# Joined read and update blocks of sample units, and a last output tile in two column groups

## Chip, cores and metric

The kernel runs as one program on the eight cores of one Trainium2 chip, written with instructions for each engine: TensorE (PE), VectorE (DVE), ScalarE (ACT), GpSimd (POOL) and the DMA queues of SyncE (SP) and GpSimd. Each core handles one of the eight prompt sequences and 16 of the 128 sample sequences; the cores don't talk to each other. The metric is the device time of the slowest core in microseconds.

## The reference

One inference step of a decoder trunk of two layers, for new prompts (2,048 tokens each, 16 learned tokens ahead of them) and for running samples (4 new tokens each). Cut to what matters:

```python
def run_layer(h, prompt, S0, ...):
    xn = rmsnorm(h, norm_g)
    q, k, v, ga, u, gb, alow, mg = jnp.split(xn @ w_in, IN_OFFSETS, axis=-1)
    la = log_sigmoid(alow @ w_alpha + b_alpha) / GATE_TAU
    # samples: one chunk of 4 tokens, starting from the stored state S0 (heads, 128, 256)
    o, S_new = gla_scan(q, k, v, la, S0, L)
    o = silu(ga) * gain * o * rsqrt(mean(o * o) + EPS)        # per head
    ya, yb = o @ w_a, (pool_mix(u) * silu(gb)) @ w_b
    s_a, s_b = split(sigmoid(mg + b_merge))
    return h + (s_a * ya + s_b * yb) @ w_out, S_new, buf_new

def gla_chunk_step(S, chunk):                                 # b: cumulated log-forget
    o = (masked q k^T with decay) @ v + (q * exp(b)) @ S      # the product with S: "read"
    S_new = exp(b_last) * S + (k * exp(b_last - b))^T @ v     # "update"

y = rmsnorm(h_last, final_norm_g)                             # after the second layer
```

The outputs are the normalised tokens of prompts and samples, and the new states of both layers.

## The kernel before

**Two phases in each layer.** Phase 1 makes the projections, the linear attention and the pooling branch of the prompt, in pairs of 128-token tiles (eight pairs; a ninth "pair" number 8 holds the 64 sample tokens and 16 learned tokens). Phase 2 goes over the pairs once more: `merge(l, j, c)` computes one of eight 128-feature chunks of the gated sum of both branches (28 matmuls of 128x128 by 256 tokens, in two PSUM banks), and `out_tile(l, j, i)` multiplies a 128-token tile by `w_out` (16 matmuls of 512 columns, in a pair of banks), adds the residual and normalises. In layer 1 it also writes the output `y`.

**The sample units.** The stored states of the 16 samples of a core are handled in phase 2, in eight units per layer; a unit takes two heads of four samples (1 MB). `sample_cast` makes a bf16 copy `S_bfm` of the loaded state (ScalarE, in two halves) and masks the keys into `kdm` (GpSimd). `sample_read` has eight matmuls, 128 rows by 32 columns by 256, four side by side in different column groups, all into the bank `bo` that four units share. `sample_write` takes four banks, runs eight matmuls of 32 rows by 128 columns by 256 (row group r into bank r), lets VectorE form `S_in * decay + bank` in eight instructions, stores the new state and asks for the load of unit u + 2.

**What sets the order.** The instructions of all engines are emitted in one list, and a planner (`Sched.list_schedule`) turns it into a queue for each engine: it runs through time with modelled costs, and each engine takes the instruction with the lowest number among those whose predecessors are done in the model. Dependencies are tracked by SBUF regions and by PSUM bank. Every engine then executes its queue strictly in that order and waits at semaphores. The sample work is cut into a list `units`; in `phase2`, after merge number k, entries are emitted as long as

```python
while done < len(units) and done * total < (k - 12) * len(units):   # total = 46
```

The list has 28 entries: opening, then cast, reads and write of eight units, two output entries, one gating entry. Banks come from `banks.one()` and `banks.pair()`, which hand out what was freed longest ago in the order of emission. Merges are numbered k = 6 to 71; of each pair from the third on, the merges c = 1 and c = 3 are followed by an output tile of the pair before.

**The end.** The last tile of layer 1 is the 64 sample tokens alone (`p == NPAIR`): 16 matmuls of 64 columns by 512 into two banks, then in two halves of 512 features on 64 partitions the residual sum, the squares with their sum, the product with the gain `fg`, then the power -1/2, the scaling (one half on ScalarE, one on VectorE) and two stores. SP closes with a wait for each DMA semaphore. Its first seven feature chunks `m3[:, kc]` may be multiplied before the last chunk's merge is through.

Lines in the profile are those of helpers: L537 is every matmul, L543 a transpose, L564 ScalarE's activation, L579, L586, L591 and L598 tensor_tensor, tensor_scalar, scalar_tensor_tensor and copies, L611 a DMA.

Of the kernel before, what the change touches and what calls it, by code (L numbers as in the profile page):

```python
# [13 lines left out]
D = 1024  # L14
# [362 lines left out]
def build_nc():  # L377
# [18 lines left out]
    gf_d = din("gfull", [NL + 1, 128, D])  # L396
    cf_d = din("cf", [128, NCF])

    y_d = dout("y", [NS + SEQ, D])
# [12 lines left out]
    with contextlib.ExitStack() as st:  # L412
# [5 lines left out]
        def f32(off, n):  # L418
            return arena[:, off // 4:off // 4 + n]
# [75 lines left out]
        bm_ = f32(v2_off + 10240, 912)  # L495
        gf = f32(v2_off + 38912, 1024)
        xnP_m = bf(v2_off + 34048, 1024)
        kd_m = bf(v2_off + 36096, 512)
# [33 lines left out]

        def mm(out, lhsT, rhs, start, stop, sgc=False, share=1.0):
            c = max(fsz(rhs) / 2.4 / share + 2.5, 28.0)
            if lhsT.dtype == F32:
                c *= 4.0
            return S.add("pe", lambda e: e.matmul(out, lhsT=lhsT, rhs=rhs, start=start, stop=stop,  # L537
                                                  skip_group_check=sgc),
                         r=[lhsT, rhs], w=[out], cost=c, lat=250.0, attach=True)

# [676 lines left out]

        def sample_read(u, bo):
            hp, j = divmod(u, 4)
            for i in range(2):  # L1220
                for r in range(4):
                    q_ = q_bd[:, (j * 4 + 2 * hp + i) * 128 + 32 * r:(j * 4 + 2 * hp + i) * 128 + 32 * r + 32]
                    mm(bank(bo)[32 * r:32 * r + 32, i * 256:(i + 1) * 256], q_,
                       S_bfm[:, (2 * r + i) * 256:(2 * r + i + 1) * 256], j + i == 0, False, sgc=True, share=4.0)

        def sample_write(l, u):
            hp, j = divmod(u, 4)
            bs = [banks.one() for _ in range(4)]
            for i in range(2):
# [81 lines left out]
        def load_h(l, k):  # L1311
            if k < 17:
                t = P2_TILES[k]
                r0, n = rows(t)
                src = hin if l == 0 else H1
                dma(hb[k % 3][0:n, :], src[r0:r0 + n, :], r=[("H1", t)] if l else [])

        def out_tile(l, j, i):
# [5 lines left out]
            m3 = V(mgT[j % 2], 8, N)  # L1324
            Wo = RR[:, (8 - N_EARLY_C) * CB:(8 - N_EARLY_C) * CB + 8192]
            h = hb[k % 3][0:n, :]
            b_ = banks.pair()
# [4 lines left out]
            y0 = 0 if t == 16 else r0 - NMETA  # L1332
            if l == 0 or p < NPAIR:
                stt(h, bank(b_)[0:n, :], 0.5, h, ALU.mult, ALU.add)
                banks.free(b_)
                if l == 0:
                    dma(H1[r0:r0 + n, :], h, w=[("H1", t)])
                    if p == NPAIR:
                        norm_t(1, h, n, k, V(xnT_m, 8, NM), True)
                    else:  # L1340
                        norm_t(1, h, n, k, V(xnO, 8, N)[:, :, i * 128:i * 128 + n])
                        if i == 1:
                            dma(XN[1][p], xnO, w=[("XN", 1, p)])
                else:
                    rs = rms(h, n, k)
                    stt(h, h, rs, fg[0:n, :], ALU.mult, ALU.mult)
                    dma(y_d[y0:y0 + n, :], h)
                load_h(l, k + 3)
                return
            s_ = ss[k % 3]  # L1350
            halves = [slice(b * 512, (b + 1) * 512) for b in range(2)]
            for b, c in enumerate(halves):
                stt(h[:, c], bank(b_)[0:n, c], 0.5, h[:, c], ALU.mult, ALU.add)
                act(xb[k % 2][0:n, c], h[:, c], AF.Square, scale=D ** -0.5, accum_out=s_[0:n, b:b + 1])
            banks.free(b_)
            hf = hb[(k + 1) % 3][0:n, :]
            for c in halves:
                tt("dve", hf[:, c], h[:, c], fg[0:n, c], ALU.mult)
            ts("dve", s_[0:n, 2:3], s_[0:n, 0:1], s_[0:n, 1:2], s2=EPS, op0=ALU.add, op1=ALU.add)
            tt("pool", s_[0:n, 3:4], s_[0:n, 2:3], nhalf[0:n, 0:1], ALU.pow)  # L1360
            for b, c in enumerate(halves):
                if b:
                    ts("dve", hf[:, c], hf[:, c], s_[0:n, 3:4])
                else:
                    act(hf[:, c], hf[:, c], AF.Copy, scale=s_[0:n, 3:4])
                dma(y_d[y0:y0 + n, c], hf[:, c])

        def phase2(l):
            dma(fg, gf_d[l + 1])
            for k in range(3):  # L1370
                load_h(l, k)
            units = [sample_open]
            box = {}

            def reads(u):
                if u % 4 == 0:
                    box[0] = banks.one()
                sample_read(u, box[0])

            for u in range(8):  # L1380
                units.append(lambda u=u: sample_cast(l, u))
                units.append(lambda u=u: reads(u))
                units.append(lambda u=u: sample_write(l, u))
                if u % 4 == 3:
# [104 lines left out]
```

How the kernel before makes its waits and increments, by code:

```python
            def run_engine(ename, eng):  # L251
                seen = {}
                for op in ops:
                    if op["eng"] != ename:
                        continue
                    need = {}
                    for d in op["kept"]:
                        sk, val = ops[d]["token"]
                        if need.get(sk, 0) < val:
                            need[sk] = val
                    items = [(sk, val) for sk, val in need.items() if seen.get(sk, 0) < val]
                    attach = items.pop() if (items and op.get("attach")) else None
                    for sk, val in items:
                        eng.wait_ge(sems[sk], val)
                        seen[sk] = val
                    inst = op["fn"](eng)
                    if attach is not None:
                        inst._wait_ge(sems[attach[0]], attach[1])
                        seen[attach[0]] = attach[1]
                    if op["token"] is not None:
                        sk, val = op["token"]
                        inst.then_inc(sems[sk], 16 if op["dma"] else 1)
                if ename == "sp":
                    for k, v in sorted(self.dma_final.items(), key=lambda kv: self.last_use[kv[0]]):
                        sk = ("dma",) + k
                        if seen.get(sk, 0) < v:
                            eng.wait_ge(sems[sk], v)
```

## Time and profile before

| what | value |
|---|---|
| time, median of 3 runs (lowest, highest) | 1153.65 us (1151.91, 1154.72) |
| the profiled execution: time | 1150.47 us |
| its span on the slowest core (core 3) | 1148.9 us |
| spans of the eight cores | 1144.4 to 1148.9 us |
| mean granted TensorE clock of the cores | 0.992 to 0.994 |
| PE busy | 1113.7 us, 97% |
| DVE, ACT, POOL busy | 610.0, 516.0, 597.9 us |

A span runs from the first to the last instruction of a core; the time of an execution holds a little more. Rows below come from the slowest core, in us from the span's start. PE is the matmul, PEld the load of its weights, which runs ahead of it.

### The profile page before, as it was taken

Reading aid. Unit: us, or ns where it says so; the run is one execution under the profiler, and the core shown is the slowest. Engines: PE = TensorE matmul, PEld = TensorE weight load, DVE = VectorE, ACT = ScalarE, POOL = GpSimd, SP = SyncE. Lnnn points to the kernel's source line nnn. Section 1 sums busy time; section 2 is a strip of 40 time slices with the busy share of each in tenths; the row PEclk is TensorE's granted clock in tenths of the full one; section 3 lists DMA queues with packets and bytes.
Section 4 is the critical chain, followed back from the end, with each engine's and each line's share of the span. In section 5 each row is a group of like instructions: output and inputs, shape, how many; then the busy total and the mean of one; then the engine's idle time right before and its main releaser. Section 6 shows DMA issues by size and latency. Waiting matters only on the chain.

```text
span 1148.9 us, 27473 instructions; the slowest of 8 cores (1144.4 to 1148.9 us)
## 1 busy us (share of the span) xinstructions
PE 1113.7 (97%) x9990; PEld 860.8 (75%) x9990; DVE 610.0 (53%) x927; ACT 516.0 (45%) x1052; POOL 597.9 (52%) x903
## 2 busy tenths in 40 slices
PE   7899999999999999999999999999999999999997
PEld 3587777777788777777767877787788777777774
DVE  5457767665642544436344776756665254544534
ACT  2545566665432333434237366555543233333333
POOL 5159788866943333333342887778785233232232
PEclk8999999999999999999999999999999999999999
DMA  9956657775697899998689224454568866655531
GB/s 191 194 110 139 137 95 150 152 159 90 94 221 146 240 276 248 249 234 223 169 162 205 56 74 90 86 84 96 99 103 195 156 197 210 222 187 172 162 102 58
DMA packets 123991, 179.06 MB, mean 156 GB/s; under 512 B 82448, under 2 KB 88976, under 8 KB 119760
## 3 DMA queue, kind: packets, MB, share of 16 engines
q1 hardware_dynamic: 108592, 141.26, 43.6%
q0 software_dynamic: 15264, 36.05, 21.9%
q8 instruction: 78, 1.28, 0.5%
q14 instruction: 57, 0.47, 0.2%
HBM read 139.87 MB, written 54.59 MB: 169 GB/s over the span
## 4 chain that ended last, share of the span: by engine, by line
PE 85%; DMA 7%; issue 2%; ACT 2%; POOL 2%; DVE 1%; SPq 0%; POOLq 0%; ACTq 0%; DVEq 0%
PE psum L537 84%; DMA arena<-sgla 2%; DMA arena<-w 2%; ACT arena L564 2%; DMA arena<-hin 2%; POOL arena L579 1%; DMA nsg_s<-arena 1%; DVE arena L591 1%; DVE arena L579 1%; POOL arena L586 0%; PE psum L543 0%; ACT L564 0%; DVE arena L586 0%; POOL arena L598 0%; SPq L611 0%
## 5 line engine op out<-in xcount | busy, mean ns | idle before, releaser
L537 PE MATMUL psum<-arena 128*128 128x256 bf16 (+6 forms) x9886 | 1109.5, 280 | 23.9 <-DMA arena<-w 6.0
L537 PEld LDWEIGHTS psum<-arena 128*128 128x128 bf16 (+2 forms) x9886 | 854.8, 98 | 273.7 <-issue 32.1
L579 POOL TENSOR_TENSOR arena<-arena 128x256 bf16<-128x256 f32 (+15 forms) x349 | 347.5, 1001 | 268.9 <-DVE arena L591 220.1
L591 DVE SCALAR_TENSOR_TENSOR arena<-arena,psum 128x256 f32<-128x256 f32 (+7 forms) x472 | 266.8, 600 | 295.4 <-PE psum L537 140.4
L564 ACT ACTIVATE arena<-psum,arena 128x256 f32<-128x256 f32 (+3 forms) x432 | 173.2, 457 | 274.0 <-PE psum L537 223.1
L586 POOL TENSOR_SCALAR arena<-arena 128x256 f32<-128x256 f32 (+6 forms) x378 | 165.2, 445 | 189.9 <-ACT arena L564 120.0
L564 ACT ACTIVATE arena<-psum 128x256 bf16<-128x256 f32 (+5 forms) x258 | 159.2, 631 | 184.8 <-PE psum L537 157.7
L564 ACT ACTIVATE arena<-arena 128x1024 bf16<-128x1024 f32 (+5 forms) x144 | 142.5, 1001 | 151.7 <-DVE arena L591 103.5
L591 DVE SCALAR_TENSOR_TENSOR arena<-arena 128x256 bf16<-128x256 f32 (+4 forms) x124 | 117.1, 952 | 53.2 <-POOL arena L579 52.2
L591 DVE SCALAR_TENSOR_TENSOR arena<-psum,arena 128x256 bf16<-128x256 f32 (+6 forms) x125 | 92.3, 760 | 78.4 <-PE psum L537 73.7
L611 POOL DMA_DIRECT2D arena<-w x106 | 62.4, 591 | 38.5 <-POOL arena L579 13.5
L579 DVE TENSOR_TENSOR arena<-psum,arena 128x512 bf16<-128x512 f32 (+4 forms) x64 | 55.1, 868 | 38.3 <-PE psum L537 22.4
L598 POOL COPY arena<-arena 128x4 f32<-128x4 f32 (+3 forms) x64 | 27.9, 442 | 48.2 <-ACT arena L564 37.0
L564 ACT ACT_TABLE_LOAD x30 | 38.5, 1283 | 18.6 <-PE psum L537 16.3
L814 DVE TENSOR_TENSOR_SCAN arena<-arena 128x1024 f32<-128x1024 bf16 (+1 forms) x18 | 39.5, 2196 | 13.1 <-ACT arena L564 13.0
L586 DVE TENSOR_SCALAR arena<-psum,arena 128x256 bf16<-128x256 f32 x64 | 28.0, 478 | 28.3 <-POOL arena L579 23.7
L564 ACT ACTIVATION_READ_ACCUMULATOR arena<-psum 128x1 f32 x136 | 27.1, 200 | 0.0
L598 DVE CAST arena<-psum 128x256 bf16<-128x256 f32 (+1 forms) x18 | 7.2, 402 | 15.8 <-PE psum L537 15.5
L543 PE MATMUL psum<-arena 128*128 128x128 bf16 (+1 forms) x104 | 8.6, 224 | 3.5 <-POOL arena L598 2.9
L543 PEld LDWEIGHTS psum<-arena 128*128 128x128 bf16 (+1 forms) x104 | 6.8, 102 | 6.1 <-POOL arena L598 3.5
L586 DVE TENSOR_SCALAR arena<-arena 128x1024 bf16<-128x1024 f32 (+6 forms) x13 | 6.6, 516 | 8.4 <-POOL arena L579 4.6
L564 ACT ACTIVATION_READ_ACCUMULATOR arena<-arena 128x1 f32 (+2 forms) x52 | 9.8, 188 | 0.0
(9 smaller groups left out, 15.0 us busy)
## 6 DMA issues: line engine op xcount, KB each, us to landing
arena<-hin SPq DMA_DIRECT2D x32, 512.0 KB, 6.9
arena<-sgla SPq DMA_DIRECT2D x16, 1024.0 KB, 8.0
nsg_s<-arena SPq DMA_DIRECT2D x16, 1024.0 KB, 8.0
arena<-w POOLq DMA_DIRECT2D x30, 512.0 KB, 14.9
arena<-w POOLq DMA_DIRECT2D x48, 224.0 KB, 5.7
arena<-XN SPq DMA_DIRECT2D x20, 512.0 KB, 6.8
H<-arena SPq DMA_DIRECT2D x16, 512.0 KB, 4.1
arena<-H SPq DMA_DIRECT2D x16, 512.0 KB, 4.4
```

What stands on the lines that cost most here:

```text
L537: return S.add("pe", lambda e: e.matmul(out, lhsT=lhsT, rhs=rhs, start=start, stop=stop, skip_group_check=sgc), r=[lhsT, rhs], w=[out], co ...
L543: return S.add("pe", lambda e: e.transpose(out, in_, ident), r=[in_, ident], w=[out], cost=c, lat=250.0, attach=True)
L564: return S.add("act", lambda e: e.activation(out=out, in_=in_, func=func, **kw), r=r, w=w, cost=c)
L579: return S.add(eng, lambda e: e.tensor_tensor(out=out, in0=in0, in1=in1, op=op), r=[in0, in1], w=[out], cost=c)
L586: return S.add(eng, lambda e: e.tensor_scalar(out=out, in0=in0, **kw), r=r, w=[out], cost=ecost(eng, fsz(out), 0.55, [out] + r))
L591: return S.add("dve", lambda e: e.scalar_tensor_tensor(out=out, in0=in0, scalar=scalar, in1=in1, op0=op0, op1=op1), r=r, w=[out], cost=eco ...
L598: return S.add(eng, lambda e: e.tensor_copy(out=out, in_=in_), r=[in_], w=[out], cost=ecost(eng, fsz(out), 0.55, (out, in_)) + (500.0 if e ...
L611: return S.add(eng, lambda e: e.dma_start(out=out, in_=in_, **kw), r=list(r) + sb_r, w=list(w) + sb_w, dma=True, after=after, cost=nb / rate)
L814: S.add("dve", lambda e: e.tensor_tensor_scan(out=B, data0=rm[:, 0:4 * n], data1=A, initial=0.0, op0=ALU.mult, op1=ALU.add), r=[rm[:, 0:4 ...
```

## The change

The read and the update of a sample unit become one entry, `sample_step`: it takes the four banks first, then emits the eight reads and the eight updates. The first read is told to the planner as also reading the whole `S_bfm` and the masked keys `kdm`, and as also writing all four update banks, so the later 15 matmuls hang on it. The list `units` has 20 entries instead of 28.

The last output tile of layer 1 gets a function of its own. The 1,024 features are halved over the partitions: features 0 to 511 of the 64 tokens on partitions 0 to 63, 512 to 1,023 on partitions 64 to 127. The matmuls are 32 of 64 columns by 256, in turn for column groups 0 to 63 and 64 to 127, in two quarters q with a bank each. The sums of squares of both partition halves are added by two FP32 matmuls with a constant 128x128 matrix `pr` that is a new input (ones where the token is the same). The residual of that tile and the final gain are loaded in the same halved layout, the gain into the region of phase 1's first weights. Scaling is by ScalarE for partitions 0 to 63 and VectorE for 64 to 127, and two stores write `y`.

```diff
+        fgl, pair_f = f32(0, 512), f32(2048, 128)
...
-        def mm(out, lhsT, rhs, start, stop, sgc=False, share=1.0):
+        def mm(out, lhsT, rhs, start, stop, sgc=False, share=1.0, also_r=(), also_w=()):
...
-                         r=[lhsT, rhs], w=[out], cost=c, lat=250.0, attach=True)
+                         r=[lhsT, rhs] + list(also_r), w=[out] + list(also_w), cost=c, lat=250.0, attach=True)
...
-        def sample_read(u, bo):
+        def sample_step(l, u, bo):
+
             hp, j = divmod(u, 4)
+            bs = [banks.one() for _ in range(4)]
+            first = dict(also_r=[S_bfm, kdm[u % 2]], also_w=[bank(b) for b in bs])
             for i in range(2):
                 for r in range(4):
                     q_ = q_bd[:, (j * 4 + 2 * hp + i) * 128 + 32 * r:(j * 4 + 2 * hp + i) * 128 + 32 * r + 32]
                     mm(bank(bo)[32 * r:32 * r + 32, i * 256:(i + 1) * 256], q_,
-                       S_bfm[:, (2 * r + i) * 256:(2 * r + i + 1) * 256], j + i == 0, False, sgc=True, share=4.0)
-
-        def sample_write(l, u):
-            hp, j = divmod(u, 4)
-            bs = [banks.one() for _ in range(4)]
+                       S_bfm[:, (2 * r + i) * 256:(2 * r + i + 1) * 256], j + i == 0, False, sgc=True, share=4.0, **first)
+                    first = {}
             for i in range(2):
                 h = 2 * hp + i
                 for r in range(4):
...
+                if t == 16 and l:
+                    for x in range(2):
+                        dma(hb[k % 3][64 * x:64 * x + 64, 0:512], src[0:NS, x * 512:(x + 1) * 512], r=[("H1", t)])
+                    return
...
+            if l and p == NPAIR:
+                return last_tile(m3, Wo, k)
...
+        def last_tile(m3, Wo, k):
+
+            h, hf, s_ = hb[k % 3][:, 0:512], hb[(k + 1) % 3][:, 0:512], ss[k % 3]
+            cs = [slice(q * 256, (q + 1) * 256) for q in range(2)]
+            for q, c in enumerate(cs):
+                b_ = banks.one()
+                for kc in range(8):
+                    for x in range(2):
+                        w_ = kc * 1024 + x * 512 + q * 256
+                        mm(bank(b_)[64 * x:64 * x + 64, 0:256], m3[:, kc, :], Wo[:, w_:w_ + 256], kc == 0, kc == 7, sgc=True,
+                           share=2.0)
+                stt(h[:, c], bank(b_)[:, 0:256], 0.5, h[:, c], ALU.mult, ALU.add)
+                act(xb[k % 2][:, c], h[:, c], AF.Square, scale=D ** -0.5, accum_out=s_[:, q:q + 1])
                 banks.free(b_)
...
+                tt("dve", hf[:, c], h[:, c], fgl[:, c], ALU.mult)
+            b_ = banks.one()
+            for q in range(2):
+                mm(bank(b_)[:, 0:1], pair_f, s_[:, q:q + 1], q == 0, q == 1)
+            ts("dve", s_[:, 2:3], bank(b_)[:, 0:1], EPS, op0=ALU.add)
             banks.free(b_)
...
+            tt("pool", s_[:, 3:4], s_[:, 2:3], nhalf[:, 0:1], ALU.pow)
+            o0, o1 = hb[k % 3][0:64, 512:1024], hb[(k + 1) % 3][64:128, 512:1024]
+            act(o0, hf[0:64, :], AF.Copy, scale=s_[0:64, 3:4])
+            ts("dve", o1, hf[64:128, :], s_[64:128, 3:4])
+            dma(y_d[0:NS, 0:512], o0)
+            dma(y_d[0:NS, 512:1024], o1)
...
+            if l:
+                for x in range(2):
+                    dma(fgl[64 * x:64 * x + 64, :], gf_d[l + 1, 64 * x:64 * x + 64, x * 512:(x + 1) * 512])
+                dma(pair_f, pr_d[:, :])
...
-                units.append(lambda u=u: reads(u))
-                units.append(lambda u=u: sample_write(l, u))
+                units.append(lambda u=u: step(u))
```

## Rows read from the trace of the kernel before

**Rows 1.** The page, busy time of the engines: us (share of the span) xinstructions.
```profile
PE 1113.7 (97%) x9990; PEld 860.8 (75%) x9990; DVE 610.0 (53%) x927; ACT 516.0 (45%) x1052; POOL 597.9 (52%) x903
```

**Rows 2.** Windows; stretch: us; PE, PEld, DVE, ACT, POOL busy (x); PEclk; DMA share; GB/s.
```profile
320.00:575.00 255.00, 254.39 (x2194) 198.71 (x2192) 111.32 (x169) 87.60 (x186) 86.72 (x134) 1.00 0.86 222
...
915.00:1111.00 196.00, 194.37 (x1606) 145.17 (x1607) 88.21 (x136) 68.25 (x142) 55.52 (x81) 1.00 0.54 178
1111.00:1149.00 38.00, 29.70 (x386) 22.26 (x383) 15.42 (x24) 12.68 (x35) 9.88 (x19) 0.92 0.21 72
```

**Rows 3.** PE's waits, 318 to 575, then 860 to 1120: total us, times, longest.
```profile
PE psum L537 <- DVE arena L591: 1.0, 2, 0.6
...
PE psum L537 <- DMA arena<-w: 1.8, 1, 1.8
```

**Rows 4.** Timeline of PE, slices about 377 us: start, duration, instruction, shape, count within slice.
```profile
376.90 0.27 PE L537 MATMUL psum<-arena 128*128 128x256 bf16 x1
...
377.11 0.29 PE L537 MATMUL psum<-arena 128*32 128x256 bf16 x4
...
377.56 0.38 PE L537 MATMUL psum<-arena 128*128 128x256 bf16 x2
```

**Rows 5.** Timeline of PE, slices about 405 us, around two left-over updates.
```profile
404.65 0.49 PE L537 MATMUL psum<-arena 128*128 128x256 bf16 x3
...
404.87 0.27 PE L537 MATMUL psum<-arena 128*128 128x256 bf16 x1
...
405.51 0.38 PE L537 MATMUL psum<-arena 128*128 128x256 bf16 x2
```

**Rows 6.** Timeline of weight loads, both phases 2: start, us, shape, count [idle before].
```profile
377.10 0.12 PEld L537 LDWEIGHTS psum<-arena 128*32 128x32 bf16 x8 [0.21 <-issue]
...
538.34 0.11 PEld L537 LDWEIGHTS psum<-arena 32*128 32x128 bf16 x2 [0.21 <-issue]
...
1088.81 0.11 PEld L537 LDWEIGHTS psum<-arena 32*128 32x128 bf16 x2 [0.21 <-issue]
```

**Rows 7.** Timeline of PE, slices of the warm-up at the start.
```profile
3.89 0.64 PE L537 MATMUL psum<-arena 32*128 32x512 bf16 x4
...
4.32 0.64 PE L537 MATMUL psum<-arena 32*128 32x512 bf16 x4
...
4.89 0.40 PE L537 MATMUL psum<-arena 128*32 128x256 bf16 x4
...
5.50 0.43 PE L537 MATMUL psum<-arena 128*32 128x256 bf16 x4
...
5.87 0.61 PE L537 MATMUL psum<-arena 128*128 128x512 bf16 x1
```

**Rows 8.** Timeline of weight loads behind the seventh unit's updates, layers 0 and 1.
```profile
518.20 12.52 PEld L537 LDWEIGHTS psum<-arena 128*128 128x128 bf16 x100 [0.89 <-DVE arena L591]
...
1067.93 4.48 PEld L537 LDWEIGHTS psum<-arena 128*128 128x128 bf16 x42 [1.04 <-DVE arena L591]
```

**Rows 9.** Timeline of all engines at the end.
```profile
1139.20 1.91 PE L537 MATMUL psum<-arena 128*64 128x512 bf16 x8 [0.41 <-POOL arena L579]
1139.31 0.32 POOL L579 TENSOR_TENSOR arena<-arena 128x64 bf16<-128x64 f32 x1 [0.16 <-DVE arena L591]
1141.00 1.28 DVE L591 SCALAR_TENSOR_TENSOR arena<-psum,arena 64x512 f32<-64x512 f32 x2 [1.84 <-PE psum L537]
...
1142.65 0.63 ACT L564 ACTIVATE arena<-arena 64x512 bf16<-64x512 f32 x1
1143.19 0.19 ACT L564 ACTIVATION_READ_ACCUMULATOR arena<-arena 64x1 f32 x1
```

**Rows 10.** Groups by line and shape, whole span: busy us, mean ns | idle before.
```profile
L591 DVE SCALAR_TENSOR_TENSOR arena<-arena,psum 128x256 f32<-128x256 f32 x259 | 108.4, 473 | 43.7 <-PE psum L537 36.1 <-POOL arena L586 3.9 <-ACT arena L564 2.9
```

**Rows 11.** Timelines of SP and of PE at the start of layer 1's phase 2.
```profile
863.80 0.34 SPq L611 DMA_DIRECT2D arena<-gfull  x1
...
915.32 2.87 PE L537 MATMUL psum<-arena 128*128 128x512 bf16 x19 [1.77 <-DMA arena<-w]
```

More of the change, by code:

```diff
@@ L397, in build_nc @@
     cf_d = din("cf", [128, NCF])
+    pr_d = din("pr", [128, 128])
     y_d = dout("y", [NS + SEQ, D])
@@ L1332, in out_tile @@
             y0 = 0 if t == 16 else r0 - NMETA
-            if l == 0 or p < NPAIR:
-                stt(h, bank(b_)[0:n, :], 0.5, h, ALU.mult, ALU.add)
-                banks.free(b_)
[L1336 to L1354, printed above, removed]
-            banks.free(b_)
[L1356 to L1366, printed above, removed]
+            stt(h, bank(b_)[0:n, :], 0.5, h, ALU.mult, ALU.add)
+            banks.free(b_)
+            if l == 0:
+                dma(H1[r0:r0 + n, :], h, w=[("H1", t)])
+                if p == NPAIR:
+                    norm_t(1, h, n, k, V(xnT_m, 8, NM), True)
+                else:
+                    norm_t(1, h, n, k, V(xnO, 8, N)[:, :, i * 128:i * 128 + n])
+                    if i == 1:
+                        dma(XN[1][p], xnO, w=[("XN", 1, p)])
+            else:
+                rs = rms(h, n, k)
+                stt(h, h, rs, fg[0:n, :], ALU.mult, ALU.mult)
+                dma(y_d[r0 - NMETA:r0 - NMETA + n, :], h)
@@ new lines, in out_tile @@
+            load_h(l, k + 3)
+        def last_tile(m3, Wo, k):
[10 more added lines that the diff above has]
+                act(xb[k % 2][:, c], h[:, c], AF.Square, scale=D ** -0.5, accum_out=s_[:, q:q + 1])
+                banks.free(b_)
+                tt("dve", hf[:, c], h[:, c], fgl[:, c], ALU.mult)
[3 more added lines that the diff above has]
+            ts("dve", s_[:, 2:3], bank(b_)[:, 0:1], EPS, op0=ALU.add)
+            banks.free(b_)
+            tt("pool", s_[:, 3:4], s_[:, 2:3], nhalf[:, 0:1], ALU.pow)
[4 more added lines that the diff above has]
+            dma(y_d[0:NS, 512:1024], o1)
@@ L1373, in phase2, with step @@
             box = {}
-            def reads(u):
+            def step(u):
                 if u % 4 == 0:
                     box[0] = banks.one()
-                sample_read(u, box[0])
+                sample_step(l, u, box[0])
             for u in range(8):
                 units.append(lambda u=u: sample_cast(l, u))
-                units.append(lambda u=u: reads(u))
-                units.append(lambda u=u: sample_write(l, u))
+                units.append(lambda u=u: step(u))
                 if u % 4 == 3:
@@ L1470 @@
         in_maps.append({
+            "pr": np.tile(np.eye(64, dtype=np.float32), (2, 2)),
             "hin": np.concatenate([xs, meta_tokens, x_prompt[c]], axis=0),
```

## The prediction

> **What bounds the kernel now.** I began with the page's totals: TensorE (PE) is busy for 97% of the span [rows 1]. A busy share does not say whether the engine does useful columns, so the next view was the busy time by stretch. The sample units run in the second phase of each layer, between 320 and 575 us and between 915 and 1111 us; there PE is busy for 254.4 of 255 and 194.4 of 196 us, while VectorE, ScalarE and GpSimd are each below half [rows 2]. PE's own waits there are almost nothing: in layer 0's phase 2 1.0 us, all for VectorE; in layer 1's the longest is 1.8 us for a weight transfer [rows 3]. So in both places the end moves with what PE's instruction stream costs, and the last stretch (1111 to 1149 us) is a chain of its own with PE busy for 29.7 of 38 us.
>
> Then I looked at how fast PE starts its instructions around the sample units, since the busy time hides slots lost in the pipeline. Full 128x256 matmuls start 0.109 us apart (one at 404.65, the second after it at 404.87 [rows 5]). Where eight read matmuls (128 rows x 32 columns, four side by side) stand between two merges, a full one starts at 376.90, the first read at 377.11 (a merge's next one would have started at 377.01), and the second full one behind them at 377.56 [rows 4]. From 376.90 to 377.56 is 0.66 us; two full slots are 0.22; the eight reads cost 0.44 us. Four side by side take one slot, so two slots, 0.22, are work. The other 0.22 is lost at the two changes of the array's shape: 0.11 each, written 0.107 below.
>
> The same holds for a piece of two. Two update matmuls left behind by their six siblings, with a full one at 404.87 and the second full one at 405.51, cost 0.64 - 0.22 = 0.42 us [rows 5]: they use the same 32 rows, run one after the other, and pay both changes. So a piece costs about 0.43 us whether it holds two matmuls or eight, and the number of pieces is what counts.
>
> The weight loads show how many there are [rows 6]: 22 pieces in layer 0 (the first 377.10, the last 538.34) and 23 in layer 1 (the last 1088.81). By kind: 16 read pieces of seven or eight, 3 of a single read whose seven siblings follow later (one slot, 0.32), 6 whole update pieces, and 10 updates broken into six and two, 20 pieces. Of these 45, 42 cost 0.425 to 0.44 and three 0.32: 42 x 0.432 + 3 x 0.32 = 19.1 us, of which only 16 x 4 x 0.109 = 7.0 us is work.
>
> **The joined blocks.** All 16 matmuls of a unit now wait at the first one and follow each other. If nothing comes between, a unit is one piece: two slots of reads, two of updates (each row group keeps its bank), and three changes: full to reads, reads to updates, updates to full. 4 x 0.109 + 3 x 0.107 = 0.757 us; 16 units make 12.1 us. That is 19.1 - 12.1 = 7.0 us less.
>
> The middle change is not in the trace at full pace. The warm-up at the start has its mirror, at half pace: updates-shaped matmuls of 512 columns start at 3.89 and 4.32 (0.43 a round), then the read-shaped ones at 4.89, 0.57 later, so 0.14 for that change; read-shaped ones of 256 columns (a round is half of 0.43) at 5.50 and full ones at 5.87, 0.37 later, so 0.15 [rows 7]. A change between two split shapes thus costs what one to the full array costs. I take 0.107. Bounds: free, -8.7 us for the blocks; double, -5.3 us. The Trainium skill's "TensorEngine Tiling (Array Packing)", Key Properties, says that changing the tiling mode drains the engine, and only changing the tile does not; by it the middle change is paid (7.0), and a reader who counted only entry and exit would have 8.7. The warm-up rows agree with it.
>
> **Stalls at the units.** At the seventh unit of each layer PE stands still after the updates: its loads idle 0.89 us in layer 0 and 1.04 in layer 1, both ended by VectorE [rows 8]; a change alone idles them 0.21 [rows 6], so 0.68 and 0.83 are stall. In the code that update was emitted after merge 49, beside an output tile that holds a pair of banks. With 20 entries in the list instead of 28, entry i is emitted after the first merge k > 12 + 46 i / 20; the seventh block then follows merge 47, where no output tile stands. These 1.5 us may go, and others may come at other units; I take half, -0.75 us, with +3 (four such stalls new) and -1.5 (both gone) as ends.
>
> **New transfers.** Two pieces of the final gain (128 KB each), a 64 KB matrix, and one transfer split in two, on SP's queue at the start of layer 1's phase 2. They target the region of the first weights, last read before the end of phase 1, so nothing on SP queues behind them for long. They stand by the gain that SP issues at 863.80; the weights for which PE waits 1.8 us come in at 915.32 [rows 11]. I cost them at nothing, covered by those 51 us; without that cover 320 KB at the 178 GB/s of layer 1's phase 2 [rows 2] is 1.8 us.
>
> **The last tile.** Before, 16 matmuls of 64 columns x 512. Eight remain after GpSimd delivers chunk 6 (PE resumes at 1139.20) and they end so that VectorE starts at 1141.00; the last chunk itself is there at 1139.31 + 0.32 = 1139.63 [rows 9]. After, pairs of 256 columns in two column groups, 16 slots of 0.109 = 1.75 us for 3.45; the 12 not waiting for chunks 6 and 7 are done before 1139.2, the last ones start at about 1139.69, and a 256-column matmul plus hand-over (0.27 [rows 4] + 0.11) gives VectorE its start at about 1140.07: -0.93 us. If the two groups don't overlap, 0.
>
> From there to the end of the second sum of squares (1143.19 + 0.19) were 2.37 us. Halved widths on 128 partitions: the addition 0.47 [rows 10] for 0.68, squares 0.42 for 0.63 (between half of it and all, as a fixed part stays): 0.47 + 0.15 hand-over, then 0.60 to the second square, then 0.51: 1.73, so -0.64. New on the path: two FP32 matmuls that add the halves over partitions, and their hand-over. No FP32 matmul is in the trace. Nearest: a bf16 one, 0.27 from start to end [rows 4]; one such is the lower bound, four plus a hand-over (1.2) the upper; I take 0.7. The power, the two scalings, two stores and SP's closing waits keep their number. Sum: -0.93 - 0.64 + 0.70 = -0.87; bounds +0.2 and -1.3.
>
> **Sum.** -7.0 - 0.75 - 0.87 = -8.6 us. The profiled execution took 1150.47 (span 1148.9, 1.6 around it), so it would take 1141.9. The median of the runs shown, 1153.65, is 3.2 above that execution; against it the forecast is 1145.0. About 0.3%, 3.5 us, can be told from no change.
>
> **Rivals.**
> *The blocks wait (slower).* Place: the first read in PE's in-order queue, which now needs both halves of the cast state, the masked keys and all four banks; before, six updates could go while a fourth bank was being emptied, and reads needed no new bank. Price: the stalls of [rows 8], 0.75 us on average, at each of 16 blocks are 12.0 us, against 7.9 of gain: 1157.8. It decides from 0.5 us a block. For: ten of 16 updates were broken, so a fourth bank is often late. Against: the planner puts the block where its model has the banks free and fills with merges; VectorE is busy 111 of 255 us [rows 2]. The Trainium skill's "TensorEngine Tiling (Array Packing)", PSUM Bottleneck, warns that packing speeds up TensorE but not the emptying of PSUM; here it would act by this wait, and the two stalls are all that bears it out. Chance 0.06.
> *The blocks break up.* The planner takes the lowest-numbered ready instruction, so matmuls emitted earlier can cut in. Two cuts in each block cost 16 x 2 x 0.21 = 6.8 us and leave the tail, so about 1152.5, no change. Against: once the first has started, the rest hang only on PE. Chance 0.08.
> *Layer 0's half is given back.* Transfers fill 0.86 of the engines' time there [rows 2]; layer 1 might then wait for weights. 7.9 / 2 = 3.9 us lost, 1145.0 + 3.9 = 1149. Against: PE waits for no transfer there [rows 3]. Layer 1, at 0.54, keeps its half. Chance 0.10.
> My case: 0.76.
>
> **Numbers.** 1145.0. Range: low end from a free middle change, both stalls gone and the tail at its lower bound (-11.5, 1142.2), less 1.2 for the spread of the runs: 1141; high end from a double change (-5.3), three us of new stalls and a tail that gives nothing (-2.3, 1151.3), cut to 1150.5, as the three would hardly meet; it takes in the third rival. My own case alone: 1141.5 to 1148. Faster by over 0.3% (under 1150.2): 0.84; within: 0.11; slower: 0.05.
>
> **What would show it.** Right: 16 pieces in the weight loads' timeline, eight a layer, each with reads and updates and about 0.76 us; PE's waits in phase 2 below 3 us; layer 0's phase 2 some 3.5 us shorter; matmuls of the last tile in pairs a few ns apart; the closing chain about 0.9 us shorter. Wrong: idle time ahead of the first read of blocks ended by VectorE, more than 16 pieces, a wait for weights at the start of layer 1, or FP32 matmuls of over 1.5 us.

## The result and the profile after

| what | before | changed |
|---|---|---|
| median of the runs (lowest, highest), us | 1153.66 (1151.91, 1154.72) | 1145.47 (1144.72, 1146.21) |
| ratio of the times, 95% interval | | 0.993 [0.9911, 0.995] |
| profiled execution: time, us | 1150.47 | 1146.21 |
| its span on the slowest core, us | 1148.9 (core 3) | 1144.6 (core 6) |
| spans of the eight cores, us | 1144.4 to 1148.9 | 1134.3 to 1144.6 |

Times here and below are medians of runs in the chip's faster state; a fourth run of the changed kernel, 1337.99 us with four cores at a mean clock of 0.81 to 0.83, is left out. The kernel became 8.2 us faster; 8.6 us were forecast. The line below is the changed kernel's page, busy time of the engines, and answers to [rows 1]: the same engine is as full as before, 7 us less busy time.

```profile
PE 1106.4 (97%) x10010; PEld 860.7 (75%) x10010; DVE 611.3 (53%) x927; ACT 516.1 (45%) x1052; POOL 605.2 (53%) x903
```

**Where the time went.** A span mixes the gain with the first phase of layer 0, which took 314 to 325 us on different cores and in different runs, with instructions that are the same in both kernels. So I cut every trace at the same instructions: the last score matmul of layer 0's phase 1, the first matmul of layer 1's decay, the last score matmul of layer 1, the first merge matmul of 64 columns (the last tile's), and the start of the last output matmul. Each number is the median of the eight cores of one profiled execution, in us; the kernels of the experiments come further below.

| kernel | layer 0, phase 2 | layer 1, phase 1 | layer 1, phase 2 | last tile's merge and matmuls | closing chain |
|---|---|---|---|---|---|
| before | 278.83 | 271.89 | 251.17 | 17.39 | 8.22 |
| changed | 275.12 | 274.02 | 244.97 | 16.47 | 8.42 |
| changed, again | 275.12 | 274.73 | 245.15 | 16.47 | 8.22 |
| blocks only | 275.12 | 272.26 | 245.04 | 17.39 | 8.58 |
| last tile only | 278.83 | 272.96 | 249.88 | 16.47 | 8.22 |
| whole pieces, not joined | 276.98 | 273.02 | 248.34 | 16.47 | 8.22 |
| blocks in turn | 276.92 | 274.24 | 246.89 | 16.47 | 8.23 |
| gain loads late | 275.12 | 272.26 | 244.97 | 16.48 | 8.48 |
| the same, again | 275.13 | 272.21 | 245.37 | 16.47 | 8.27 |
| pooling load after transposes | 275.12 | 272.71 | 245.00 | 16.47 | 8.58 |
| loads late, sums apart | 275.12 | 272.25 | 246.10 | 16.47 | 7.85 |
| all three | 275.13 | 272.49 | 245.13 | 16.47 | 8.20 |

From before to changed the columns say -3.70, +2.13, -6.21, -0.92 and +0.20; with +0.94 in the first stretch that is -7.6 us. The second, a loss, was not forecast.

**The units.** The next rows are the weight loads of the changed kernel around the first unit (start, us, shape, count [idle before]), the answer to [rows 6].

```profile
384.86 0.12 PEld L539 LDWEIGHTS psum<-arena 128*32 128x32 bf16 x8 [0.42 <-issue]
385.19 0.12 PEld L539 LDWEIGHTS psum<-arena 32*128 32x128 bf16 x8 [0.21 <-issue]
385.52 1.09 PEld L539 LDWEIGHTS psum<-arena 128*128 128x128 bf16 x11 [0.21 <-issue]
```

The reader is to see eight reads, eight updates right behind them, and full matmuls, with 0.33 us from each to the next: two slots of 0.109 and one change. (A slot is the time from one full 128x256 matmul's start to the next.) In both layers there are eight such blocks, all whole and in the order read, update. By the starts of the matmuls a block costs 0.767 us, eight of them 6.14 us in layer 0 and 6.13 in layer 1. The 22 and 23 pieces of before cost 10.17 and 10.85 us, of which 0.76 and 1.13 were the stalls behind the seventh units.

**Waits.** PE's waits in the changed kernel (us in all, times, longest): first layer 0's phase 2, then from 860 us on, as in [rows 3].

```profile
PE psum L539 <- ACT arena L566: 1.0, 1, 1.0
PE psum L539 <- DMA arena<-OT: 0.3, 1, 0.3
...
PE psum L539 <- DVE arena L593: 2.8, 1, 2.8
PE psum L539 <- DVE arena L581: 0.4, 1, 0.4
```

The stalls behind the seventh units are gone, as in every kernel here whose list has 20 entries; the kernels with 28 entries keep them. A wait for ScalarE is new on the two slowest cores (1.0 us on core 6, 0.7 on core 5), but no core had it when the changed kernel ran again. One more wait is new and lies behind the window shown: 0.3 us for GpSimd at about 590 us, close to the end of layer 0's phase 2. All eight cores have it in the changed kernel, none in the kernel before. The 2.8 us are new too, and lie at the very end of layer 1's phase 1, not in phase 2. The windows answer to [rows 2] (stretch: us; PE, PEld, DVE, ACT, POOL busy; clock; DMA share; GB/s):

```profile
320.00:575.00 255.00, 253.69 (x2209) 200.37 (x2207) 112.65 (x172) 88.71 (x189) 91.75 (x139) 1.00 0.93 226
910.00:1106.00 196.00, 195.94 (x1654) 149.96 (x1653) 89.64 (x138) 70.23 (x146) 59.64 (x84) 1.00 0.53 186
```

In layer 1's phase 2 PE is busy for 195.9 of 196 us and starts 1654 matmuls where it started 1606: the slots that the changes of shape took are filled, and so is the wait for weights of 1.8 us that the window of before holds. In layer 0's the transfers now fill 0.93 of their time instead of 0.86.

**The loss in layer 1's phase 1.** SP's queue in the changed kernel at the end of that phase (start, us to issue, operation):

```profile
840.91 1.25 SPq L618 DMA_TRANSPOSE arena<-arena  x1
842.82 0.50 SPq L613 DMA_DIRECT2D arena<-gfull  x1
843.48 0.48 SPq L613 DMA_DIRECT2D YP<-arena  x1
846.08 0.32 SPq L613 DMA_DIRECT2D arena<-YP  x1
847.06 1.24 SPq L618 DMA_TRANSPOSE arena<-arena  x1
```

And the same stretch of the kernel before:

```profile
841.82 1.22 SPq L616 DMA_TRANSPOSE arena<-arena  x1
843.76 0.32 SPq L611 DMA_DIRECT2D YP<-arena  x1
845.85 0.32 SPq L611 DMA_DIRECT2D arena<-YP  x1
847.38 1.22 SPq L616 DMA_TRANSPOSE arena<-arena  x1
```

The load of the gain (gfull) stands between the last transposes of phase 1, 21 us ahead of the place in [rows 11] next to which I had put it: its target, the region of the first weights, is free early, and the planner used that. It pushes the pooling branch's store (YP<-arena) and load (arena<-YP, 256 KB) back, so that the load is issued 0.98 us ahead of the last transpose instead of 1.53. The issues' view has that transpose's time to landing, in the changed kernel:

```profile
arena<-arena SPq DMA_TRANSPOSE x1, 7.3
```

before:

```profile
arena<-arena SPq DMA_TRANSPOSE x1, 3.0
```

The waits of the changed kernel between 850 and 866 us show who stood behind it:

```profile
POOL arena L581 <- DMA arena<-arena: 3.9, 1, 3.9
DVE arena L593 <- POOL arena L581: 2.9, 1, 2.9
PE psum L539 <- DVE arena L593: 2.8, 1, 2.8
```

The transpose holds GpSimd's gate product, that holds VectorE, and that holds PE. The two rows are of different cores: on core 6 the landing rose from 4.6 to 7.3 us, on core 3 from 3.0 to 6.1. Over the eight cores it took 3.0 to 4.6 us before (mean 3.7) and 4.6 to 7.3 after (mean 5.9), and PE's wait there, by the starts of its matmuls, rose from 0 to 1.6 us on average, 3.7 at most. How far ahead the load is issued does not settle it alone: with 0.98 us on core 6 the transpose landed in 7.3 us, with 1.01 on core 7 in 4.8.

**The end.** The changed kernel's last tile on the slowest core, the answer to [rows 9]:

```profile
1135.34 0.89 PE L539 MATMUL psum<-arena 128*64 128x256 bf16 x8 [0.82 <-POOL arena L581]
1135.44 0.32 POOL L581 TENSOR_TENSOR arena<-arena 128x64 bf16<-128x64 f32 x1 [0.16 <-DVE arena L593]
...
1136.23 0.76 DVE L593 SCALAR_TENSOR_TENSOR arena<-psum,arena 128x256 f32<-128x256 f32 x2 [0.93 <-PE psum L539]
...
1137.73 0.19 ACT L566 ACTIVATION_READ_ACCUMULATOR arena<-arena 128x1 f32 x1
...
1137.97 1.01 PE L539 MATMUL psum<-arena 128*128 128x1 f32 x4 [1.74 <-ACT arena L566]
1139.15 0.16 DVE L588 TENSOR_SCALAR arena<-psum 128x1 f32<-128x1 f32 x1 [1.50 <-PE psum L539]
...
1140.10 0.72 ACT L566 ACTIVATE arena<-arena 64x512 f32<-64x512 f32 x1 [2.19 <-POOL arena L581]
```

From PE's resuming to VectorE's start are 0.89 us for 1.80. From there to the end of the second sum are 1137.92 - 1136.23 = 1.69 us for 2.38. From there to the scaling are 2.18 us, where it was 1.09. The same chain on core 4:

```profile
1131.08 0.61 PE L539 MATMUL psum<-arena 128*128 128x1 f32 x4 [1.74 <-ACT arena L566]
1131.86 0.16 DVE L588 TENSOR_SCALAR arena<-psum 128x1 f32<-128x1 f32 x1 [1.10 <-PE psum L539]
...
1132.80 0.72 ACT L566 ACTIVATE arena<-arena 64x512 f32<-64x512 f32 x1 [1.78 <-POOL arena L581]
```

Here the four FP32 passes take 0.61 us, on the slowest core 1.01. The windows of PE on the slowest core, in those passes and in the stretch before (stretch, its length, busy time (count), granted clock, DMA share, GB/s):

```profile
1137.90:1139.00 1.10, 1.01 (x4) 0.50 0.03 7
1130.00:1134.00 4.00, 4.00 (x124) 1.00 0.34 135
```

On core 4 the passes ran at 1.00. Four cores (1, 2, 3 and 6) were at 0.50, which is 1.2 of 2.4 GHz, and four at 1.00, all after the same 1.74 us without a matmul. On the first four the granted clock fell within that pause; on the others it fell too, but only behind the FP32 passes.

### The profile page after: what moved, and what is told of

Read it like the earlier page. It is cut to its first block, busy times and chain, and to the rows that moved or that the text cites. A ratio compares the mean times of both kernels' runs of the same rounds, so it can differ in the third digit from the quotient of the medians.

```text
span 1144.6 us, 27587 instructions; the slowest of 8 cores (1134.3 to 1144.6 us)
## 1 busy us (share of the span) xinstructions
PE 1106.4 (97%) x10010; PEld 860.7 (75%) x10010; DVE 611.3 (53%) x927; ACT 516.1 (45%) x1052; POOL 605.2 (53%) x903
## 4 chain that ended last, share of the span: by engine, by line
PE 80%; DMA 9%; issue 3%; POOL 3%; ACT 2%; DVE 2%; POOLq 0%; SPq 0%; DVEq 0%; ACTq 0%
PE psum L539 80%; DMA arena<-w 3%; ACT arena L566 2%; DMA arena<-arena 2%; POOL arena L581 2%; DVE arena L593 1%; DMA nsg_s<-arena 1%; DMA arena<-sgla 1%; DMA arena<-hin 1%; DMA OT<-arena 1%; POOL arena L588 1%; DVE arena L581 1%; DMA arena<-OT 0%; POOL arena L600 0%; PE psum L545 0%
## 5 line engine op out<-in xcount | busy, mean ns | idle before, releaser
L581 POOL TENSOR_TENSOR arena<-arena 128x256 bf16<-128x256 f32 (+14 forms) x349 | 353.9, 1020 | 265.4 <-DVE arena L593 209.8
L566 ACT ACTIVATE arena<-arena 128x1024 bf16<-128x1024 f32 (+4 forms) x144 | 141.7, 997 | 157.4 <-DVE arena L593 102.9
L588 DVE TENSOR_SCALAR arena<-arena 128x1024 bf16<-128x1024 f32 (+5 forms) x12 | 6.3, 532 | 7.3 <-POOL arena L581 3.3
L566 ACT ACTIVATION_READ_ACCUMULATOR arena<-arena 128x1 f32 (+1 forms) x52 | 9.8, 188 | 0.0
```

Source lines behind the costliest of these rows:

```text
L566: return S.add("act", lambda e: e.activation(out=out, in_=in_, func=func, **kw), r=r, w=w, cost=c)
L581: return S.add(eng, lambda e: e.tensor_tensor(out=out, in0=in0, in1=in1, op=op), r=[in0, in1], w=[out], cost=c)
L588: return S.add(eng, lambda e: e.tensor_scalar(out=out, in0=in0, **kw), r=r, w=[out], cost=ecost(eng, fsz(out), 0.55, [out] + r))
```

## The experiments

My theory of the gain was that it is the price of the changes of the array's shape, saved by fewer pieces. The rival: what helps is that a unit waits for everything at its head, so that nothing is left behind or stalls; joining reads and updates would then add little. My theory of the loss was that the loads of the final gain stand in SP's queue; the rival: the joined blocks shift PE's work so that the transposes meet other transfers.

**One part alone.** The first kernel is before with only the joined blocks (the end of its edit is shown); the second has the new last tile and its loads, with reads and updates apart.

```diff
-                units.append(lambda u=u: reads(u))
-                units.append(lambda u=u: sample_write(l, u))
+                units.append(lambda u=u: step(u))
```

> Only the joined blocks; the last tile, its loads and its transfers as before. Theory 1, the gain is the number of shape changes on TensorE: 16 pieces of about 0.77 us in place of 45 worth 19.1 us plus 1.9 us of stalls, so layer 0's second phase 3.5 to 4 us shorter, layer 1's 4 to 5 us shorter, its first phase unchanged at about 272 us (no gain loads in SP's queue), the closing part unchanged: 7.5 to 9 us faster than before, 1145 to 1146 us. Rival, the gain comes from the last tile or from transfers that moved: then this kernel is within 3 us of before, above 1150 us.

> Only the new last tile with its loads; reads and updates of the sample units apart as before. Theory 1: 45 pieces of 19 us as before, both second phases as before up to the closing part. The closing part gives 0.5 us, and the gain loads in SP's queue cost about 2 us at the end of layer 1's first phase (274 us in place of 272), partly given back where the wait for weights after it was: 0 to 2 us slower than before, 1153.5 to 1155.5 us. Rival, the loads are harmless and the first phase of layer 1 was lengthened by what the shorter layer 0 moved: 0.5 us faster than before, first phase at 272 us.

Measured beside the same runs of before (median 1150.89): blocks only 1143.62 us, 0.9929 [0.9905, 0.9952]; last tile only 1150.44 us, 0.9997 [0.9982, 1.0012]. So the gain is the blocks'. In the stages, the blocks alone give both phases 2 (275.12 and 245.04) and leave layer 1's phase 1 at 272.26; the last tile alone, with its loads, has 272.96 there, and the last transpose lands after 5.2 us on average instead of 3.7 (blocks only: 4.0). It gains 0.92 in its matmuls and loses 1.1 in phase 1; its time came out as the rival had it, not 2 us slower as my theory had, because only half of the 2 us was lost and layer 1's phase 2 was 1.3 us shorter in this execution (see the waits for weights below). The loss goes with the loads, but not with them alone: with the blocks of before it is 1.1 us (272.96, and 273.02 in the next kernel), with joined blocks 2.1 to 2.8 in the three executions that have both (274.02, 274.73, 274.24). Why joining raises it is not shown.

**Whole pieces, not joined.** The second kernel of above, with the first read waiting for all of the cast state and the first update for all four banks and the keys:

```diff
 def sample_read(u, bo):
+    first = dict(also_r=[S_bfm])
...
 def sample_write(l, u):
+    first = dict(also_r=[kdm[u % 2]], also_w=[bank(b) for b in bs])
```

> The changed last tile; reads and updates apart as before, but the first read waits for the whole cast state and the first update for all four banks, so that neither can be broken up by a bank. Theory 1, by pieces: 10 left-over pairs of updates vanish, 45 pieces become 35 (a lone first read may still be cut off), 10 x 0.43 = 4.3 us less than with the last tile alone and about 2.7 us more than the changed kernel: 1148 to 1150 us. Rival, that waiting for all four banks costs what it saves: TensorE stalls of 0.5 us or more ahead of updates, time as with the last tile alone, 1153 us or above.

Measured: 1149.01 us beside 1150.89, 0.9981 [0.9968, 0.9994]. Two rows of its weight loads, an update piece and a later one:

```profile
441.04 0.12 PEld L539 LDWEIGHTS psum<-arena 32*128 32x128 bf16 x8 [0.42 <-ACT arena L566]
...
468.70 0.12 PEld L539 LDWEIGHTS psum<-arena 32*128 32x128 bf16 x8 [0.21 <-issue]
```

Nearly every piece holds eight now; there are 17 and 18, at 8.43 and 8.74 us. That is 17.2 us against 21.0 of before and 12.3 joined: 3.9 of the 8.7 us come from pieces that are no longer broken (ten left-over pairs less), the other 4.9 from joining: 35 pieces with two changes each against 16 with three are 22 changes, 2.4 us, and the rest is mainly one update in each layer that took 1.56 us with a stall. The stages agree: layer 0's phase 2 gains 1.85 of 3.70. Both theories hold a half. Without the stalls (1.9 us in all before, 2.25 here, none joined) the split of the 8.7 us is 4.2 for whole pieces, 2.6 for joining and 1.9 for the stalls. Waiting at the head brought no new stall: one in each layer, at the seventh unit, as before.

**Two more changes in each block.** The changed kernel with the block in the order four reads, four updates, four reads, four updates: the same matmuls and waits, five changes of shape for three.

```diff
             for i in range(2):
+                h = 2 * hp + i
                 for r in range(4):
...
                     mm(bank(bo)[32 * r:32 * r + 32, i * 256:(i + 1) * 256], q_,
...
-            for i in range(2):
-                h = 2 * hp + i
                 for r in range(4):
...
                     mm(bank(bs[r])[:, i * 256:(i + 1) * 256], kdm[u % 2][p_, i * 128:(i + 1) * 128],
```

> The changed kernel with the 16 matmuls of a block in another order: four reads, four updates, four reads, four updates. The same work, banks, waits and number of pieces (16), but five changes of shape in a block in place of three. Theory 1, each change costs 0.107 us whichever two shapes meet: a block costs 0.77 + 0.21 = 0.98 us, both second phases are 1.7 us longer, 3.4 us in all: 1149 us, about 0.4% faster than before. Rival, what counts is the number of pieces or the wait ahead of them, and changes between two split shapes are free: same as the changed kernel, 0.77 us a block.

Measured: 1148.99 us beside 1152.78, 0.996 [0.9945, 0.9976]. Its weight loads show one block without the full matmuls' load in between:

```profile
409.06 0.77 PEld L539 LDWEIGHTS psum<-arena 128*32 128x32 bf16 x16 [0.21 <-issue]
```

By the starts a block costs 0.991 us, 0.224 more than 0.767: 0.112 for each change between the two split shapes. Sixteen blocks make 3.6 us, and the two phases 2 are 1.80 and 1.92 us longer than the changed kernel's. This is the direct price of a change. The Trainium skill's "TensorEngine Tiling (Array Packing)", Key Properties, which says that a change of tiling mode drains the engine, gives no price; this run shows one, for a change between two split modes, and it is that of a change to the full array.

**The loads late.** The changed kernel with the loads of the gain and of `pr` taken from the head of phase 2 to merge 40 of layer 1; the queues of PE, VectorE, ScalarE and GpSimd stay the same.

```diff
-            if l:
-                for x in range(2):
-                    dma(fgl[64 * x:64 * x + 64, :], gf_d[...])
-                dma(pair_f, pr_d[:, :])
...
+                if l and k == 40:
+                    at = [S.last()]
+                    for x in range(2):
+                        dma(fgl[64 * x:64 * x + 64, :], gf_d[...], after=at)
+                    dma(pair_f, pr_d[:, :], after=at)
```

> The changed kernel with the halved gain and the pairing matrix loaded in the middle of layer 1's second phase, behind merge 40, in place of its start. The queues of TensorE, VectorE, ScalarE and GpSimd are the same; SP's alone differs. Theory, the loads push the transfers of the pooling output against the last transpose of layer 1's first phase: that phase takes 272 us in place of 274, the last transpose lands in 3 to 4.6 us, TensorE's wait behind it (up to 3.7 us on the slowest cores) is gone; some 1 us may come back as a wait for weights after it. 1 to 2 us faster than the changed kernel, 1144 us. Rival, the wait comes from elsewhere: same as the changed kernel, 1145.8 us, first phase at 274.

> The kernel with late gain loads once more beside it: 0.8 to 0.9% faster than before, 5 us faster than the blocks in turn; layer 1's first phase at 272 us.

Measured: 1141.66 us beside 1150.89, 0.9913 [0.9897, 0.993]; again, on another chip, 1143.03 beside 1152.78, 0.991 [0.9893, 0.9927]. Layer 1's phase 1 is back at 272.26 and 272.21 us, and in the second of these runs the transpose of SP's queue is again 1.53 us behind the load of YP and lands in 3.0:

```profile
846.61 0.32 SPq L613 DMA_DIRECT2D arena<-YP  x1
848.14 1.22 SPq L618 DMA_TRANSPOSE arena<-arena  x1
```

So the forecast that these transfers cost nothing failed by their place; the 0.3 us that are left above the 271.89 of before stand in the kernel with blocks only too. The average landing was 4.2 and 3.9 us; in the first run one core still had 7.2 us and a wait of 2.7, so the loads make late landings frequent and are not the only thing that can.

**The load of YP behind the transposes.** Is it the gain's load itself that slows the transpose, or the load of YP that it pushed up to it? The changed kernel, its gain loads in place, with that load made to wait for the last transposes:

```diff
-            dma(y_, YP[p], r=[("YP", p)])
+            dma(y_, YP[p], r=[("YP", p)], after=last_t[-3:] if l and j == 0 else ())
```

> The changed kernel once more, as the mark for the three that run beside it: 0.6 to 0.8% faster than before; last transpose of layer 1's first phase landing in 4.5 to 7.5 us, that phase at 273 to 275 us.

> The changed kernel with its gain loads where they are, but the load of the pooling output that stands just ahead of the last transpose in SP's queue issued just behind it. Theory, the gain loads act by pushing that 256 KB load against the transpose: it lands in about 3 us on all cores, TensorE's wait behind it is gone, layer 1's first phase takes 271.5 to 272.3 us, 1.5 to 2.5 us faster than the changed kernel. Rival, the gain transfers themselves or the weights from GpSimd's queue slow it: it lands in 4.5 us or more on most cores as in the changed kernel and nothing is won.

SP's queue of this kernel:

```profile
842.47 0.51 SPq L613 DMA_DIRECT2D arena<-gfull  x1
843.14 0.46 SPq L613 DMA_DIRECT2D YP<-arena  x1
846.75 1.22 SPq L620 DMA_TRANSPOSE arena<-arena  x1
849.98 0.32 SPq L613 DMA_DIRECT2D arena<-YP  x1
```

Beside before at 1153.01 us, the changed kernel took 1147.26, 0.9945 [0.9925, 0.9965], and this one 1146.78, 0.9941 [0.9922, 0.996]. The times can't be told apart, but the place can: the mean landing fell from 6.0 to 4.0 us, PE's mean wait from 2.0 to 0.4, and the stage from 274.73 to 272.71. My forecast for this kernel, about 3 us on all cores and a gain in time, missed: the even cores still landed in 4.5 to 5.7 us. But with the gain's loads in place, moving the load of YP behind the transpose took most of the loss away, so it is this load close ahead that slows the transpose, and the gain's load is the push. A load in flight beside it is not enough: before, with 1.5 us between them, it was still under way when the transpose was issued (it landed after 2.6 to 2.9 us), and the transposes took 3.7 us on average. Why the even cores land in some 4.5 us and the odd ones in some 3.0, even before, stays open.

**The two sums apart.** In the last tile the first FP32 matmul needs only the first square, yet it starts after the second: both partial sums lie in one tracked piece of memory. With the loads late, the sums in two tiles:

```diff
+            sq = [ss[k % 3], ss[(k + 1) % 3]]
...
-                act(..., accum_out=s_[:, q:q + 1])
+                act(..., accum_out=sq[q][:, 0:1])
...
-                mm(bank(b_)[:, 0:1], pair_f, s_[:, q:q + 1], q == 0, q == 1)
+                mm(bank(b_)[:, 0:1], pair_f, sq[q][:, 0:1], q == 0, q == 1)
```

> Gain loads late, and the two partial sums of squares in places of their own, so that the first FP32 matmul need not wait for the second square. Against the kernel with late loads alone the closing part is shorter by one FP32 matmul, two of the four passes of 0.22 us: 0.4 us; against the changed kernel 2.4 us in all. If the FP32 matmuls' latency and not their number sets it, 0 to 0.2 us.

> Late gain loads, sums apart, and the pooling load behind the last transpose: layer 1's first phase at 271.5 to 272 us on all cores; 2.5 to 3.5 us faster than the changed kernel, about 1.0% faster than before. If a load behind the transpose delays the merges that read it, the wait shows up at the first merges of layer 1's second phase and the gain over the kernel with late loads alone is none.

Measured, same chip (before 1153.01): 1143.64 us, 0.9921 [0.9899, 0.9943]; with the YP load behind the transposes as well 1144.12, 0.992 [0.9902, 0.9937]. PE at the end of the first of them, on core 0:

```profile
1125.10 0.89 PE L539 MATMUL psum<-arena 128*64 128x256 bf16 x8 [0.82 <-POOL arena L581]
1127.13 0.78 PE L539 MATMUL psum<-arena 128*128 128x1 f32 x4 [1.14 <-ACT arena L566]
```

PE stands still for 1.14 us instead of 1.74; the closing chain is 7.85 us. On cores at full clock in both it is 0.42 less than with late loads alone (8.27), as forecast; the medians, 0.42 and 0.63 apart, also hold cores at half clock, whose number changes from run to run (three here in part or in whole, five and two in the runs with late loads alone). With all three edits it was 8.20: there, as with blocks only and in the kernel with the late YP load, one short VectorE instruction of the chain started 0.35 us later than the rows around it explain, which I can't place. The forecast of 271.5 to 272 us on all cores for layer 1's phase 1 missed there: four cores had 272.1 and the even ones 272.9 to 274.5. The 0.4 us does not show in the times. The version with late loads alone has the lowest ratio, 0.991 in both of its runs, against 0.993 and 0.9945 for the changed kernel. The intervals overlap a little; what carries that verdict is the stage, 1.8 to 2.5 us shorter. Against the versions with the sums apart or with blocks only the times decide nothing.

## Why the prediction was right, and where it was not

**The blocks** (predicted 19.1 - 12.1 = 7.0 us): 12.27 us measured, by 16 blocks of 0.767 for 0.757, and 19.1 before without the stalls, so 6.9 us. The middle change, the unknown of the sum, cost 0.106 in the changed kernel (0.215 from the first read of the last round to the first update, less a slot) and 0.112 in the run with two more; that it costs what the others do had been taken from the half-paced warm-up. Free (-8.7) and double (-5.3) are both excluded. What the gain consists of can be counted in the rows: 90 changes became 48, some 4.5 us at 0.107 each, and 87 slots became 64, some 2.5 us, since left-over matmuls take slots of their own; both are estimates from [rows 4] to [rows 6].

**The stalls** (-0.75 taken, -1.5 and +3 as ends): both are gone, 1.9 us by the starts, on every core and in every kernel with joined blocks. That is more than the end of -1.5, which had been read from the idle time of the weight loads (0.68 and 0.83 us) where the starts show 0.76 and 1.13. In layer 0, 22 pieces at 10.17 less 6.14 should give 4.0; the stage gave 3.7. The difference is the new wait of 0.3 us for GpSimd at the end of that stage, which all kernels with joined blocks have on all cores and the kernels with reads and updates apart have on none; why is not shown.

**The new transfers** (nothing): this step failed. I gave as reasons that nothing on SP queues behind them for long and that they would stand by the gain of [rows 11], covered by 51 us until the next wait. They stood 21 us earlier, and the cost was not a wait for them but the landing of a transpose that met another load: 2.1 us in the median, up to 3.7 us of PE's time on a core. My bound of 1.8 us, from the bytes and the rate, was the wrong mechanism at nearly the right size.

**The last tile** (-0.87): -0.91 in the matmuls (-0.93 predicted), -0.69 in addition and squares (-0.64), +0.69 for the FP32 matmuls on a core at full clock (+0.70), but +1.10 on the slowest, at half clock. By the stages -0.92 + 0.20 = -0.72. So the mechanism held and the term that the sum did not have is the half clock on four cores, 0.40 us there. The upper bound of +0.2 does not follow from its terms: with 0 for groups that don't overlap and 1.2 for the FP32 matmuls they give +0.56. The two column groups do run side by side: matmuls of a pair start 3 ns apart.

**What was not in the sum.** Layer 1's phase 2 gained 6.2 us, of which the blocks and the stall explain 10.85 - 6.13 = 4.7. The other 1.5 are the wait for weights of [rows 3]: seven of eight cores had it in the execution of before (0.5 to 1.8 us), one in the changed kernel's. But it had come back on four cores when the changed kernel ran again, and the kernel with late loads had it on one and then on four, so it belongs to the execution and not to the change. Core 0 of before, the one without that wait, shows it: its stage took 249.69 us, 4.72 more than the 244.97 of the changed kernel's cores without a wait, which is what the blocks and the stall give. The two cores in the middle of before's eight had waits of 1.1 and 1.5 us. By the mechanism both phases 2 thus gained 3.7 + 4.7 = 8.4 us for 7.75 forecast.

**The rivals.** *The blocks wait*: the longest wait in layer 0's phase 2 is 1.0 us, on one core and not ahead of a block, against 0.75 us at each of 16 blocks; it fell. *The blocks break up*: 16 of 16 are whole; it fell. *Layer 0's half is given back*: 3.7 of it was kept, though transfers rose to 0.93 of their time; layer 1 did lose 2 us to a transfer, but at a transpose in phase 1, which no rival had. So the number came out near partly by luck: the loss of 2.1 us, which the sum did not have, met a larger gain at the stalls and, in the profiled executions, the 1.5 us of waits for weights.

## What to carry to other kernels

Count the changes of the array's shape rather than the small matmuls: here each costs as much as a slot of 256 columns, whichever shapes it lies between. Keep a group whole first: that was worth 4.2 us here, joining two groups 2.6 (and the stalls that went with it 1.9). When a load is given a target that is free early, look up where the planner will put it in the queue, not where it is written, and ask what it pushes together there; an `after` on work that runs well before the data is needed takes it out of the way. Before a last chain is shortened by a pass through an idle TensorE, price that pass at half clock too.

## What the runs showed of the hardware

- A change between two split shapes of the array costs 0.112 us at full clock, the same as one to or from the full array (0.107).
- The last transpose of SP's queue in that phase landed in 3.7 us (mean of the eight cores) with a 256 KB load issued 1.5 us ahead of it, in 5.9 with the load 0.5 to 1.0 us ahead, and in 4.0 with the load behind it. Cores with the same lead differ (4.8 and 7.3 us at 1.0 us), so the lead is not all of it.
- An FP32 matmul of one column shows as two passes in the trace (four rows for two matmuls), which start 0.11 to 0.14 us apart at full clock and 0.21 to 0.24 at half; four took 0.61 and 1.01 us.
- TensorE's granted clock was 0.50 in those passes on four of eight cores and 1.00 on the others, after the same pause of 1.74 us. The Trainium skill's "TensorE: Matmul & The Clock Gate", What's actually happening, says that the clock follows how busy the engine has been recently; these rows agree that it falls when the engine stands idle, and show that the pause's length alone does not decide whether it falls within it.
